# Transposing the activations of routed experts by VectorE and GpSimd instead of TensorE

## The reference, cut to what matters

```
def _swiglu(h, w_gate, w_up, w_down):
    return (jax.nn.silu(h @ w_gate) * (h @ w_up)) @ w_down
```

## Time and profile before

| | |
|---|---|
| median of 3 runs | 1582.07 us (1580.07 to 1582.33) |
| profiled execution | 1582.01 us, of which the span from the first to the last instruction is 1580.2 us |
| granted TensorE clock, mean | 0.999 |
| busy over the span | PE 99%, PEld 83%, DVE 77%, ACT 62%, POOL 17% |
| chain that ended last | PE 94%, DVE 2%, ACT 2%, POOL 1% |

### The profile page before, as it was taken

The page is one execution under the profiler, slowest core; times in us unless marked ns, Lnnn a source line. Parts: engine busy times, 40 slices in busy tenths (PEclk is TensorE's granted clock), DMA queues, the critical chain, the costliest instruction groups (busy, mean ns, idle before and its releaser), DMA issues.

```text
span 1580.2 us, 23620 instructions
## 1 busy us (share of the span) xinstructions
PE 1565.6 (99%) x9486; PEld 1306.9 (83%) x9486; DVE 1211.2 (77%) x825; ACT 981.9 (62%) x732; POOL 271.4 (17%) x244
## 2 busy tenths in 40 slices
PE   9999999999999999999999999999999999999997
PEld 8788889999988888888888888888888888888886
DVE  5556566555557758888888888888888888888897
ACT  5443444333454357777777777777777777777775
POOL 5599315300037108100000000000000000000100
PEclk9999999999999999999999999999999999999999
DMA  9644647855511368999999999999999999999993
GB/s 350 173 159 154 207 147 286 282 200 186 186 54 57 115 247 317 394 391 365 386 363 365 384 367 362 386 365 363 382 373 350 379 376 356 388 374 356 397 393 143
DMA packets 202143, 469.18 MB, mean 297 GB/s; under 512 B 7784, under 2 KB 20288, under 8 KB 202064
## 3 DMA queue, kind: packets, MB, share of 16 engines
q1 hardware_dynamic: 199872, 461.13, 80.7%
q0 software_dynamic: 2048, 6.88, 1.4%
q10 hardware_dynamic: 144, 0.07, 0.0%
HBM read 461.23 MB, written 15.21 MB: 302 GB/s over the span
## 4 chain that ended last, share of the span: by engine, by line
PE 94%; DVE 2%; ACT 2%; POOL 1%; issue 1%; DMA 0%; ACTq 0%; DVEq 0%; POOLq 0%
PE PS L1744 90%; PE PS L1862 2%; DVE weights_lo L1263 1%; ACT weights_hi L884 1%; POOL b_padded L784 1%; PE PS L2075 0%; ACT c_padded L884 0%; PE PS L2234 0%; DVE residual L1263 0%; POOL param_tmp L643 0%; DMA constants<-in_constants 0%; PE PS L1832 0%; ACT x_transposed_hi L934 0%; DVE act_rows L1263 0%; POOL param_tmp L640 0%
## 5 line engine op out<-in xcount | busy, mean ns | idle before, releaser
L1263 DVE TENSOR_TENSOR weights_lo<-weights_raw,weights_hi 128x2048 fp32r<-128x2048 f32 (+1 forms) x419 | 962.0, 2305 | 256.6 <-ACT weights_hi L884 255.0
L884 ACT ACTIVATE weights_hi<-weights_raw 128x2048 fp32r<-128x2048 f32 (+1 forms) x419 | 800.8, 1912 | 364.7 <-PE PS L1744 353.4
L1744 PE MATMUL PS<-weights_hi,gathered_hi 128*128 128x512 f32 x896 | 355.2, 396 | 0.3 <-DVE gathered_lo L1625 0.3
L1744 PE MATMUL PS<-weights_hi,gathered_lo 128*128 128x512 f32 x896 | 355.2, 396 | 0.0
L1744 PE MATMUL PS<-weights_lo,gathered_hi 128*128 128x512 f32 x896 | 352.2, 393 | 0.0
L1744 PE MATMUL PS<-weights_hi,act_transposed_hi 128*128 128x512 f32 x624 | 253.0, 405 | 0.3 <-DVE act_transposed_lo L1422 0.3
L1744 PE MATMUL PS<-weights_hi,act_transposed_lo 128*128 128x512 f32 x624 | 247.0, 396 | 0.0
L1744 PE MATMUL PS<-weights_lo,act_transposed_hi 128*128 128x512 f32 x624 | 245.7, 394 | 0.0
L1744 PEld LDWEIGHTS PS<-weights_hi,gathered_lo 128*128 128x128 f32 x896 | 168.2, 188 | 41.3
L1744 PEld LDWEIGHTS PS<-weights_lo,gathered_hi 128*128 128x128 f32 x896 | 168.2, 188 | 41.2
L1744 PEld LDWEIGHTS PS<-weights_hi,gathered_hi 128*128 128x128 f32 x896 | 168.2, 188 | 39.9 <-DVE gathered_lo L1625 0.4
(11 more groups left out here) (283 smaller groups left out, 1273.3 us busy)
## 6 DMA issues: line engine op xcount, KB each, us to landing
weights_raw<-in_moe_w_up SPq DMA_DIRECT2D x111, 1024.0 KB, 7.2
weights_raw<-in_moe_w_down SPq DMA_DIRECT2D x111, 1024.0 KB, 6.9
weights_raw<-in_moe_w_gate SPq DMA_DIRECT2D x110, 1024.0 KB, 7.1
weights_raw<-in_ret_w_in SPq DMA_DIRECT2D x24, 1024.0 KB, 6.7
weights_raw<-in_ffn_w_gate SPq DMA_DIRECT2D x14, 1024.0 KB, 5.1
weights_raw<-in_ffn_w_up SPq DMA_DIRECT2D x14, 1024.0 KB, 5.1
weights_raw<-in_ffn_w_down SPq DMA_DIRECT2D x14, 1024.0 KB, 4.9
weights_raw<-in_ret_w_out SPq DMA_DIRECT2D x8, 1024.0 KB, 4.9
```

The lines of the kernel that those rows point to most:

```text
L884: return nc.scalar.activation(o, i, ACT.Copy)
L1263: return nc.vector.tensor_tensor(o, a, b, op)
L1744: return nc.tensor.matmul(o, l, r, start=start, stop=stop)
```

## The change

In experts 1 to 7, for steps 0 to 5 of the seven, the transposes are taken from TensorE. VectorE, after its product, waits for it and transposes `act_rows[:, 0]` in blocks of 32x32 into `act_rows[:, 1]`. GpSimd moves the blocks to their places with 16 copies of 32 partitions x (4 x 32) elements into `silu_of_gate[:, 1]`, in four groups of four with a wait for the group's last copy between groups. ScalarE and VectorE make `act_transposed_hi` and `act_transposed_lo` from there, one unit later than before (unit 6s+7, and 8 for step 0). TensorE waits for the product (`mult_done`) instead of `act_lo` before the next up units. Expert 0, the seventh step of each expert, the dense layer and the second pass (which doesn't run with these inputs) stay as they were. GpSimd's gather of rows for the last sum now stands behind the moves of step 1 of the last expert, with a wait for its landing.

```diff
+        def turned_off_pe(e, s):
+            return s < STEPS - 1 and e is not None and not is_first(e)
+        def blocks_moved_by(e, s):
+            return count(s + 2 - STEPS, e, STEPS - 1)
+        def turned_on_pe(p, e, s):
+            if p:
+                return count(STEPS + EXPERTS - 1 + s + 1, e, STEPS)
+            return s + 1 if is_first(e) else count(STEPS, e, 1)
+        def evacuated_at(off_pe):
+            return {(8 if off_pe else 7) if s == 0 else 41 if s == STEPS - 1 else 6 * s + (7 if off_pe else 6): s
+                    for s in range(STEPS)}
...
 GpSimd:
-            pool.wait_ge(y_sent, 16 + 16 * LAST)
-            rows_come_back(0)
+            def move_blocks(e, s):
+                pool.wait_ge(blocks_turned, blocks_moved_by(e, s))
+                moved = act_rows[:, 1, :].rearrange("p (f j c) -> p f j c", f=FT, j=4)
+                act_t = gated[:, 1, :].rearrange("p (f c) -> p f c", f=FT)
+                for shift in range(4):
+                    for i in range(4):
+                        j = (i + shift) % 4
+                        ins = nc.gpsimd.tensor_copy(act_t[32 * j:32 * j + 32, :, 32 * i:32 * i + 32],
+                                                    moved[32 * i:32 * i + 32, :, j, :])
+                    if shift < 3:
+                        link(ins)
+                ins.then_inc(blocks_moved, 1)
+                pool.wait_ge(blocks_moved, blocks_moved_by(e, s))
+            for e in range(1, EXPERTS):
+                for s in range(STEPS - 1):
+                    move_blocks(e, s)
+                    if e == LAST and s == 1:
+                        pool.wait_ge(y_sent, 16 + 16 * LAST)
+                        rows_come_back(0)
+                        pool.wait_ge(rows_back, 64)
...
 ScalarE, ffn:
+                        if p == 0 and turned_off_pe(e, evac_at[i]):
+                            act.wait_ge(blocks_moved, blocks_moved_by(e, evac_at[i]))
+                            copy(ht_hi[evac_at[i] % 2][:, 0, :, :],
+                                 gated[:, 1, :].rearrange("p (f c) -> p f c", f=FT)).then_inc(act_hi, 1)
...
 VectorE, ffn:
                         tt(act_rows[:, 0:tts, :], gated[:, 0:tts, :], PS[:, tts:2 * tts, :], ALU.mult).then_inc(mult_done, 1)
+                        if p == 0 and turned_off_pe(e, mult_at[i]):
+                            dve.wait_ge(mult_done, count(s + 1, e, STEPS))
+                            nc.vector.transpose(act_rows[:, 1, :], act_rows[:, 0, :]).then_inc(blocks_turned, 1)
...
+                            act_t = gated[:, 1, :] if p == 0 and turned_off_pe(e, evac_at[i]) else PS[:, tts + t, :]
...
 TensorE, ffn:
-                    if s0 + s:
+                    if s and p == 0 and turned_off_pe(e, s - 1):
+                        pe.wait_ge(mult_done, count(s0 + s, e, STEPS))
+                    elif s0 + s:
                         pe.wait_ge(act_lo, count(s0 + s, e, STEPS))
...
-                    turn(s)
+                    if not (p == 0 and turned_off_pe(e, s)):
+                        turn(s)
```

More of the change, by code:

```diff
@@ L401, in trunk @@
         act_t_done = sem("act_transposed")
+        blocks_turned = sem("act_blocks_transposed")
+        blocks_moved = sem("act_blocks_moved")
         act_hi = sem("act_hi_ready")
@@ L964, in ffn @@
                 silu_at = {ffn_first(s) + 4: s for s in range(STEPS)}
-                evac_at = {7 if s == 0 else 41 if s == STEPS - 1 else 6 * s + 6: s for s in range(STEPS)}
+                p = s0 // (STEPS * (1 + EXPERTS))
+                evac_at = evacuated_at(p == 0 and not is_first(e))
                 for i in range(FFN_UNITS):
@@ L975, in ffn @@
                         s = s0 + evac_at[i]
-                        act.wait_ge(act_t_done, count(s + 1 - STEPS, e, STEPS))
-                        copy(ht_hi[evac_at[i] % 2][:, 0:tts, :, :],
-                             PS[:, tts:2 * tts, :].rearrange("p t (f c) -> p t f c", f=FT)).then_inc(act_hi, 1)
+                        if p == 0 and turned_off_pe(e, evac_at[i]):
+                            act.wait_ge(blocks_moved, blocks_moved_by(e, evac_at[i]))
+                            copy(ht_hi[evac_at[i] % 2][:, 0, :, :],
+                                 gated[:, 1, :].rearrange("p (f c) -> p f c", f=FT)).then_inc(act_hi, 1)
+                        else:
+                            act.wait_ge(act_t_done, turned_on_pe(p, e, evac_at[i]))
+                            copy(ht_hi[evac_at[i] % 2][:, 0:tts, :, :],
+                                 PS[:, tts:2 * tts, :].rearrange("p t (f c) -> p t f c", f=FT)).then_inc(act_hi, 1)
                     if each:
@@ L1357, in ffn @@
                         dve.wait_ge(used, count(u0 + ffn_first(mult_at[i]) + 4, e, FFN_UNITS))
-                        if s > STEPS:
-                            dve.wait_ge(act_t_done, count(s - STEPS, e, STEPS))
+                        if s > STEPS and not is_first(e) and mult_at[i] == 0:
+                            dve.wait_ge(act_t_done, turned_on_pe(p, e - 1, STEPS - 1) if p or not isinstance(e, int) or e > 1
+                                        else STEPS)
+                        elif s > STEPS and (p or is_first(e)):
+                            dve.wait_ge(act_t_done, turned_on_pe(p, e, mult_at[i] - 1))
                         tt(act_rows[:, 0:tts, :], gated[:, 0:tts, :], PS[:, tts:2 * tts, :], ALU.mult).then_inc(mult_done, 1)
+                        if p == 0 and turned_off_pe(e, mult_at[i]):
+                            dve.wait_ge(mult_done, count(s + 1, e, STEPS))
+                            nc.vector.transpose(act_rows[:, 1, :], act_rows[:, 0, :]).then_inc(blocks_turned, 1)
                     if i in evac_at:
@@ L1365, in ffn @@
                         for t in range(tts):
-                            ins = tt(ht_lo[b][:, t, :, :], PS[:, tts + t, :].rearrange("p (f c) -> p f c", f=FT),
+                            act_t = gated[:, 1, :] if p == 0 and turned_off_pe(e, evac_at[i]) else PS[:, tts + t, :]
+                            ins = tt(ht_lo[b][:, t, :, :], act_t.rearrange("p (f c) -> p f c", f=FT),
                                      ht_hi[b][:, t, :, :].bitcast(F32), ALU.subtract)
@@ L1938, in ffn @@
                             half0()
-                        if s == 1 and half == 0:
+                        if s == 1 and half == 0 and not (p == 0 and turned_off_pe(e, 0)):
                             turn(0)
-                    if s0 + s:
+                    if s and p == 0 and turned_off_pe(e, s - 1):
+                        pe.wait_ge(mult_done, count(s0 + s, e, STEPS))
+                    elif s0 + s:
                         pe.wait_ge(act_lo, count(s0 + s, e, STEPS))
```

## The result

The changed kernel takes 1842.34 us (median of six runs, 1838.89 to 1843.45) against 1582.20 us of the kernel before on the same chip (six runs, 1580.07 to 1583.09): 1.164 times as long, 95% interval 1.1631 to 1.1656. That is 260 us more; 229 were forecast, and 1842 lies in the range. The page of the changed kernel, against the earlier trace rows: busy time, clock in 40 slices, the chain's shares and four groups of instructions (name, count, busy us, mean ns, idle before and its releaser).

A forecast was written before the change was run, and what follows sets the result against it. The prediction took TensorE, busy 99% of the span, to bound the kernel. Steps growing from 17.24 to 22.7 us, times 42, add 229 us to 1582.01: 1811 us, chance 0.42, range 1664 to 1950.

The forecast's parts named there:

- What comes off TensorE: Four transposes in each of 42 steps leave TensorE, 0.435 us a step: 18.3 us is all there is to gain.
- VectorE's transpose: VectorE's 128x512 transpose of its product in blocks: 0.7 us, bounds 0.4 and 1.4, worth -13 and +29 us.
- The copy: Each of GpSimd's 16 copies a step: 0.32 us, one every 0.30; bounds 0.24 and 0.45 give 1764 and 1887 us.
- The lock: GpSimd's copies and VectorE's weights_lo subtractions exclude each other on SBUF; VectorE holds it 13.7 us of a 16.8 us step.
- The walk: One step followed engine by engine, one copy entering each gap, 14 running alone: 22.7 us a step against 17.24.
- rival 2: TensorE's clock falls in the idle gap, one unit at 1.2 GHz: +88 us more, 1899 us; chance 0.18.
- How the copies are spread over the gaps matters little: In a stalled step VectorE's work, GpSimd's copies and ScalarE's copy come one after another, whatever the spread; no size given.
- The joint of two experts: Seventh steps unchanged and step 0 taken like the others: a middle expert of some 154 us.
- Overlapping copies: GpSimd's copies of a group overlap, a group costing 0.32 to 0.5 us: 1664 to 1694 us; chance 0.28.
- Copies unhindered: GpSimd's copies pass beside the subtractions, TensorE stays the bound at 16.80 us a step: 1563.7 us; chance 0.09.
- Cancelled gain: Overlap and luck in the gaps cancel the gain: no change; chance 0.03.
- The row gather: In the last expert, GpSimd's gather behind the step 1 moves takes some 16 us within a 22 us step: costs nothing.

The follow-up runs named there:

- experiment 2: Changed kernel without the block moves, GpSimd answering each transpose with one tiny memset: 1567.24 us, 0.9908 of the kernel before.
- experiment 7: Changed kernel with small filler products in TensorE's idle gap (24 behind step 0, 10 behind step 1, 16 behind steps 2 to 5): 1799.16 us.
- experiment 5: Changed kernel with GpSimd starting a step's copies only after the last weights_lo subtraction ahead of the evacuation: 1924.18 us.
- experiments 9: Changed kernel with 8 copies on GpSimd and 8 on ScalarE (2, 3, 3), steps 1 to 5 only, evacuation at unit 8: 1592.05 us.
- 11: Changed kernel with 8 copies on GpSimd, 8 on ScalarE in two later lots of four, steps 1 to 5 of experts 1 to 6: 1622.95 us.
- experiments 3: Changed kernel with only two of the four copy groups made (8 copies of 16): 1693.13 us, 1.0706 of the kernel before.
- 6: Changed kernel with the evacuation of steps 1 to 5 one unit later, at unit 6s+8: 1797.49 us, 1.1359 of the kernel before.
- experiment 1: Changed kernel with GpSimd's copies replaced by memsets of the same places: 1572.87 us, 0.995 of the kernel before.
- 9 to 12: Four runs sharing the changed kernel's copies, GpSimd and ScalarE: 8+8, 1592.05 us; 6+10, 1601.38; 8+8 in two later lots, 1622.95; 10+6 likewise, 1655.90.

## Why the prediction was right, and where it wasn't

**What comes off TensorE** (18.3 us): experiment 2 has 15 us, the rest being lost at the joints of the experts (a middle expert gives 2.4 us and not 6 x 0.435, the last one 0.4). Right in kind and nearly in size.

**VectorE's transpose** was taken at 0.7 us and took 0.71 (710 to 715 ns), hidden in experiment 2. ScalarE's copy out of SBUF: 0.63 for 0.6.

**The copy**: 0.29 us, one every 0.33, where 0.32 and 0.30 were taken. Start to start counts, and it was 10% too low.

**The lock**, on which the forecast rested, was there: 120 of 672 copies took 1 to 2.45 us, memsets none. The few rows sufficed to see it. The forecast held it for the whole recorded instruction, though, and it is about 0.15 us shorter (last section).

**The walk** gave 22.7 us a step. The measured 22.8 of the calmest steps agrees by two errors that cancel. It let one copy into each gap and left 14 to run alone. At full clock (experiment 7) 12 run alone. The last subtraction ends 17.1 us behind the evacuation's end where the walk had 17.8, from there to the next evacuation it is 4.2 us for 4.4 (fewer copies, but 0.33 each), and the step is 21.95. On top comes the clock, which the forecast had left to rival 2: in a step of 22.8 the last subtraction ends 1.5 us later still, each of the last three has a gap of about 0.5 us before it (in experiment 7 two run back to back), six copies get through and 10 run alone. So the step's error was -0.75 us for the gaps and the walk's times, and +0.87 for the clock. That they cancel is luck. In the same way TensorE's idle stretch, forecast at some 6 us, is 2.9 to 4.2 us in the middle experts' steps 2 to 5, most likely because its units end later at the lower clock.

**"How the copies are spread over the gaps matters little" is the step that failed.** It is worth 82 us by experiment 5; experiments 9 and 11, which differ in where ScalarE's lots stand (and in that 11 leaves the last expert as it was, which helps it), are 31 us apart, in part through a copy that does or doesn't make a gap. The reason given (all comes one after another) forgot that VectorE's gaps exist anyway, so a copy inside one is free. In the forecast itself it hid two copies a step (12 alone where 14 were reckoned), 0.66 us a step or 28 us in all, and the clock covered that up.

**The joint of two experts** was taken like any step. From the seventh step's evacuation to the next expert's first is 32.6 us instead of 23.7, but the interval before it is 2 to 3 us shorter: in sum 5.7 to 7.0 us more. The next interval, of the first step, is 19.8 against 13.0. With four steps in between that are 5.3 to 6.5 longer this makes 158.2 us and more an expert where 154 was forecast.

**Rivals.** Overlapping copies (0.28) fall: no two copies of GpSimd in a step of the changed kernel or of experiments 3, 5, 6, 9 and 11 start less than 0.32 us apart, though in 9 and 11 the order of the partitions is another. The Trainium skill, GPSIMD Engine Reference, Instruction dispatch, lets each of GpSimd's cores go on by itself; if that happens here, it doesn't show in these rows. The clock (0.18) was not an alternative to the forecast but an addition to it: the idle stretches of 2.9 to 5.9 us lower it in every expert, at 43 us where 88 were reckoned. The Trainium skill's warning of idle gaps between bursts (TensorE: Matmul & The Clock Gate, Why this matters for your kernels) agrees. Copies unhindered (0.09) falls with the lock; nearest to it is experiment 1, whose memsets are quicker than copies: 1573 us for the 1563.7 reckoned. Cancelled gain (0.03) falls with the 260 us. The row gather cost GpSimd one wait of 7.6 us, as reckoned in kind (16 us in a step of 22).

## What to carry to other kernels

Before moving work to an idle engine, look in the trace for any place where the two engines already ran beside each other: a few rows at the program's start forecast 229 of the 260 us, with two errors against each other. Where one engine holds a lock for most of a step, count the gaps and how many instructions begin in each; what the step pays for is the instructions that are left when the last gap is over, 0.33 us each here. Whether fewer and larger moves would have paid, no run shows. And an idle engine isn't a free one when everything waits for its last instruction: 16 x 0.33 us against 0.44 us on TensorE had to be hidden entirely to gain anything.

## What the runs showed of the hardware

- The lock ends about 0.15 us before the copy's recorded end. In the changed kernel and experiments 3, 6, 7 and 9 to 12, a subtraction that began 0.13 us or more behind the start of a copy of 0.29 us that wasn't held took its usual 2.29 us (179 cases, to 3 ns). One that began less than 0.035 us behind took 0.11 to 0.13 longer (44 cases; 2.41 us at 1011.72 above). In the other direction a held copy of the changed kernel ends about 0.15 us behind the subtraction.
- GpSimd's memset of 32x128 took 0.198 us and passed beside subtractions; a copy of the same, not held, took 0.287.
- A 32x128 copy costs ScalarE 0.31 us and the next starts 0.32 behind it, while its 128x512 evacuation, four times the elements on a partition, costs 0.63. GpSimd's copy of 32 elements took 0.24 us and of 128 elements 0.29. So on either engine most of a small copy's price is not its elements.
- A step of 22.5 to 23.8 us with one idle stretch of 2.9 to 4.2 us has a mean TensorE clock of 0.85 to 0.93 of 2.4 GHz. The clock falls after the stretch: in the step shown, products run at full clock for about 1 us when they resume at 1106.84, then at 1.2 GHz for 3.4 us.
